# Seating the dilated heads in opposite halves of the partitions, and moving the rotation's angles to the first layer's down products

## The chip, the cores and the metric

One core of one Trainium2 chip. The metric is the device time of one execution in microseconds: the whole program, from the loading of the inputs to the writing of the output. Lower is better.

## The reference, cut to what matters

Two transformer blocks of two layers each, on 256 tokens of width 1024, in float32. The first block (called A in the kernel) has three kinds of attention and a gated feed-forward; the second (B) has pooling, a convolution, a dilated attention, a cross attention to a memory, and a feed-forward. What the change touches is the dilated attention of B and the rotation of its queries and keys:

```python
HEAD_DIM = 64
DIL_CONFIGS = ((128, 1), (512, 4), (2048, 16))
HEADS_PER_GROUP = 4
...
def rope_tables(positions):
    inv = ROPE_THETA_2 ** (-jnp.arange(0, ROT_DIM, 2, dtype=jnp.float32) / ROT_DIM)
    ang = positions.astype(jnp.float32)[..., None] * inv
    return jnp.cos(ang)[:, :, None, :], jnp.sin(ang)[:, :, None, :]
...
def dilated_attention(q, k, v):          # 12 heads: 3 groups of 4
    ...
    def block(bi):                       # 128 queries at a time
        for g, (window, dil) in enumerate(DIL_CONFIGS):
            ...                          # keys t, t - dil, ..., t - window; those before 0 masked out
            sc = jnp.einsum("bhqd,bhqkd->bhqk", qb[g], kk).astype(jnp.float32) * scale
            m = jnp.max(sc, axis=-1, keepdims=True)
            p = jnp.exp(sc - m)
            den = jnp.sum(p, axis=-1, keepdims=True)
            o = jnp.einsum("bhqk,bhqkd->bhqd", p, vv.astype(jnp.float32)) / den
            lses.append(m + jnp.log(den))
        wts = jax.nn.softmax(jnp.stack(lses, axis=0), axis=0)
        return jnp.sum(wts * jnp.stack(outs, axis=0), axis=0).astype(q.dtype)
```

Head h of the result mixes head h of each of the three groups, so the kernel takes those three together as one softmax over all their keys.

## The kernel before, in words

The activations lie with features on the partitions and tokens in the free dimension. Every weight is streamed once per layer through five raw buffers, in chunks of up to 128x1536 words, in an order fixed by hand. ScalarE copies a chunk to a rounded high part (`weights_hi`, `split_hi`, L641), VectorE subtracts that from the raw chunk to get the low part (`weights_lo`, `split_lo`, L652) and so frees the raw buffer for SP's next transfer. Four pairs of high and low parts are held. TensorE makes each product as three matmuls per 128x128 block of weights (L787, L789, L790: high by low, low by high, high by high), and frees a pair of parts when it leaves its chunk; ScalarE's split of the chunk four places later waits for that.

Each engine walks the same list of steps, `order_a` for the layers of block A and `order_b` for those of B, and issues its own share of each step. A step `("job", name)` is one product; on VectorE and ScalarE it begins with the splits up to two chunks beyond the job's last one. So what stands ahead of a job in the list stands ahead of its splits on VectorE.

In block A the attention runs as ten pairs of heads: `pair_in(i)` is the scores of pair i and, on TensorE, the turning of the probabilities of pair i - 1 (L1130, L1140), `pair_out(i)` the values of pair i - 2 (L1156). Behind pair_out 8, 9 and 10 stand the products `part0`, `part1`, `part2` (the output projection, as far as its inputs are there). Ahead of `part0` stands `("angles", 0)`: in layer 0, `vector_angles` (L2621 on) turns the positions to float and works out the angles of block B's rotation, reduced to -pi..pi, in a chain of instructions on 128x256 of which each waits for the one before. Their results lie in `ANG` and `TURNS` (named sin_dil and cos_dil in the trace) until ScalarE takes the sines at the end of block A. The last products of a layer are `down0` to `down3`, 44 blocks of weights each; behind each of them VectorE adds the product to x (L1714). The chunk borders of `down2` and `down3` run through without a cut, so `down2` is three full chunks and two thirds of a fourth.

In block B the queries and keys of the twelve dilated heads lie in `QKB` (qk_b): twelve tiles of 256 columns, six of queries and six of keys, and in each tile two heads, one in partitions 0 to 63 and one in 64 to 127. Head f (group g, head h: f = 4g + h) lies in tile f // 2, half f % 2. The sixteen score steps (eight per layer: head h, query block m) stand between the twelve `gate` products. A step makes three matmuls with a contraction of 64 (`tensor_dil_scores`, L1915), one for each group: 128 queries by the keys seen so far, 128 of them for m = 0 and 256 for m = 1. All three have f % 2 = h % 2. Groups 0 and 1 go to the first score bank and group 2 to the second. Then VectorE scales and masks them into `PB` (L1961), ScalarE takes the exponentials, VectorE divides, TensorE turns the result (L1927) and multiplies it with the values (L1943), each a step later:

```python
            for g in range(NG):
                f = g * DH + h
                r = slice((f % 2) * DHD, (f % 2 + 1) * DHD)
                ins = nc.tensor.matmul(dil_scores(h, m, g), QKB[r, f // 2, m * P:(m + 1) * P],
                                       QKB[r, 6 + f // 2, 0:dil_tiles(m) * P], start=True, stop=True)
```

`dil_columns` says which columns of w_in make up a tile of `QKB`: the sixteen turned elements of both heads stand together in the middle of the partitions. The weights are laid out so on the host.

Of the kernel before, what the change touches and what calls it, by code (L numbers as in the profile page):

```python
# [15 lines left out]
P = 128  # L16
DM = 1024
T = 256
QT = T // P
# [30 lines left out]
NG = len(DILS)  # L50
DH, DHD = 4, 64
# [23 lines left out]
def dil_columns(first, tile):  # L75

    turned = [(r + half * ROT // 2, 1) for r in range(ROT // 2) for half in range(2)]
    heads = [first + (2 * tile + half) * DHD for half in range(2)]
    return [(heads[0] + ROT, DHD - ROT)] + [(h + r, n) for h in heads for r, n in turned] + [(heads[1] + ROT, DHD - ROT)]


def constants():
# [45 lines left out]
    return at, np.ascontiguousarray(np.concatenate(list(cols.values()), 1))  # L128

# [272 lines left out]
def transformer(nc, known, stream_a, jobs_a, stream_b, jobs_b, const_at,  # L404
                x_in, mem_in, pos_in, w_a, w_b, gains_a, gains_b, consts, out):
    ctx = ExitStack()
    with ctx:
# [122 lines left out]
        QKB = b1.place("qk_b", (12, T))  # L530
# [7 lines left out]
        PB = b1.place("probs_b", (NG, QT, P))  # L538
# [42 lines left out]
        score_bank = [ctx.enter_context(nc.psum_tensor(f"scores{i}", [P, PAIR], F32)) for i in range(2)]  # L581
# [440 lines left out]
        n = KF // 2 - 1  # L1022
        order_a += [("ffn_hi", n - 1), ("ffn_in", n), ("ffn_lo", n - 1), ("ffn_out", n), ("ffn_hi", n), ("ahead", f"up{n}"), ("ffn_lo", n)]
        order_a += [("job", "down0"), ("root_table", "down")] + [("job", f"down{i}") for i in range(1, 4)]

# [623 lines left out]
        def vector_a(dve, l):  # L1649
# [4 lines left out]
            for kind, name in order_a:  # L1654
# [4 lines left out]
                if kind == "front":  # L1659
                    tag, i = name  # L1660
# [12 lines left out]
                elif kind == "angles":  # L1673
                    if l == 0:
                        vector_angles(dve)
# [29 lines left out]
                elif kind == "job":  # L1705
# [5 lines left out]
                    elif name[0] == "o" or name.startswith("down"):  # L1711
                        i = int(name[-1])
# [178 lines left out]
        def dil_tiles(m):  # L1891

            return m + 1

        def dil_scores(h, m, g):

            w = dil_tiles(m) * P
            return score_bank[g // 2][:, (g % 2) * w:(g % 2 + 1) * w]

# [4 lines left out]
        def tensor_dil_scores(pe, l, i):  # L1904
            s = B
            h, m = D_STEPS[i]
            if i == 0:
                pe.wait_ge(*s.at(l, "qk_rope", 2))
                pe.wait_ge(*s.at(l, "values", "v0"))
            else:  # L1910
                pe.wait_ge(*s.at(l, "dil_masked", i - 1))
            for g in range(NG):
                f = g * DH + h
                r = slice((f % 2) * DHD, (f % 2 + 1) * DHD)
                ins = nc.tensor.matmul(dil_scores(h, m, g), QKB[r, f // 2, m * P:(m + 1) * P],  # L1915
                                       QKB[r, 6 + f // 2, 0:dil_tiles(m) * P], start=True, stop=True)
            ins.then_inc(*s.mark("dil_scores", i))
# [30 lines left out]
        def vector_dil(dve, l, i):  # L1948
# [7 lines left out]
            mask = const_b("mask").rearrange("p (g k n) -> p g k n", g=NG, k=QT)  # L1956
            for g0, gn in ((0, 2), (2, 1)):
                src = score_bank[g0 // 2][:, 0:gn * kts * P].rearrange("p (g n) -> p g n", g=gn)
                dst = PB[:, g0:g0 + gn, 0:kts, :].rearrange("p g k n -> p g (k n)")
                mk = mask[:, g0:g0 + gn, QT - kts:QT, :].rearrange("p g k n -> p g (k n)")  # L1960
                ins = nc.vector.scalar_tensor_tensor(out=dst, in0=src, scalar=DHD ** -0.5, in1=mk, op0=ALU.mult, op1=ALU.add)  # L1961
# [658 lines left out]

        def vector_angles(dve):  # L2621

            dve.wait_ge(loaded["pos"], 16)
            nc.vector.tensor_copy(ANG[:, :], POS[:, :]).then_inc(*O.mark("angle", 0))
            dve.wait_ge(*O.at(0, "angle", 0))
            nc.vector.tensor_scalar(ANG[:, :], ANG[:, :], const("inv_freq"), None, ALU.mult).then_inc(*O.mark("angle", 1))
# [131 lines left out]
```

## Time and profile before

| | |
|---|---|
| median of 3 runs | 1678.62 us |
| lowest, highest | 1677.86, 1681.99 us |
| the profiled execution | 1683.09 us, its span 1681.3 |
| TensorE matmul busy | 1641.5 us (98%) |
| TensorE weight load busy | 1585.0 us (94%) |
| VectorE, ScalarE, GpSimd busy | 1202.8, 900.3, 113.7 us |
| HBM read | 271.13 MB, 162 GB/s over the span |
| granted TensorE clock, mean | 0.995 |

The profile is one execution of the program. An engine's busy time is the time in which it executes an instruction; TensorE's matmuls overlap, so the distance from the start of one to the start of the next says more than the duration of one. A row of a timeline gives the start, the time covered, the engine, the line, what it writes and reads, how many records were merged, and in brackets the idle time before it with what ended it. A float32 matmul leaves two records, one for each pass. The rows of fp32r products (L787, L789, L790) leave one.

### The profile page before, as it was taken

How to read it: one execution, taken by the hardware profiler on the slowest of the kernel's cores; microseconds unless marked ns; L12 is line 12 of the kernel's file. 1: busy time of each engine (PE TensorE's matmuls, PEld its weight loads, DVE VectorE, ACT ScalarE, POOL GpSimd, SP SyncE). 2: the span in 40 equal slices, each digit the busy share in tenths (PEclk: the TensorE clock that was granted, in tenths of full speed). 3: DMA queues.
4: the chain of work that ended last, by engine and by line, in shares of the span. 5: the costliest groups of instructions: out<-in, count | busy, mean ns of one | idle time of the engine just before them, and what ended most of it. 6: DMA issues, size and time to landing. Idle time of an engine off the chain costs nothing.

```text
span 1681.3 us, 31825 instructions
## 1 busy us (share of the span) xinstructions
PE 1641.5 (98%) x13566; PEld 1585.0 (94%) x13566; DVE 1202.8 (72%) x1765; ACT 900.3 (54%) x1378; POOL 113.7 (7%) x72
## 2 busy tenths in 40 slices
PE   9989999999999999999999999999999999999997
PEld 9978999999789999989999989999999999999997
DVE  5887777556977776477858768983677768679863
ACT  5585644454675444544545665544445446655542
POOL 2020000020110000210000110001200001110000
PEclk9999999999999999999999999999999999999999
DMA  8313555553225555555335435554454345345550
GB/s 294 109 59 114 196 197 189 173 194 126 95 86 183 202 201 182 211 203 189 114 134 189 136 125 195 198 193 165 165 197 162 132 155 184 120 151 207 197 184 34
DMA packets 53406, 275.03 MB, mean 164 GB/s; under 512 B 6288, under 2 KB 6928, under 8 KB 53136
## 3 DMA queue, kind: packets, MB, share of 16 engines
q1 hardware_dynamic: 52544, 271.15, 46.3%
q8 instruction: 107, 1.75, 0.4%
q10 hardware_dynamic: 720, 1.84, 0.3%
q14 instruction: 35, 0.29, 0.0%
HBM read 271.13 MB, written 1.05 MB: 162 GB/s over the span
## 4 chain that ended last, share of the span: by engine, by line
PE 75%; DVE 16%; ACT 5%; issue 2%; POOL 1%; DMA 0%; ACTq 0%; SPq 0%; DVEq 0%; POOLq 0%
PE bank L787 16%; PE bank L789 15%; PE bank L790 15%; DVE weights_lo L652 4%; PE scores L787 3%; PE scores L789 3%; PE scores L790 3%; PE heads L787 2%; PE heads L790 2%; PE heads L789 2%; ACT weights_hi L641 1%; DVE x_lo L934 1%; PE scores L1915 1%; ACT probs L1205 1%; PE heads L1943 1%
## 5 line engine op out<-in xcount | busy, mean ns | idle before, releaser
L652 DVE TENSOR_TENSOR weights_lo<-raw,weights_hi 128x1536 fp32r<-128x1536 f32 (+2 forms) x344 | 583.8, 1716 | 226.8 <-ACT weights_hi L641 226.4
L641 ACT ACTIVATE weights_hi<-raw 128x1536 fp32r<-128x1536 f32 (+4 forms) x352 | 499.9, 1440 | 179.5 <-PE bank L790 82.7
L787 PE MATMUL bank<-x_hi,weights_lo 128*128 128x256 f32 (+1 forms) x1588 | 443.7, 279 | 2.5 <-DVE weights_lo L652 2.1
L789 PE MATMUL bank<-x_lo,weights_hi 128*128 128x256 f32 (+1 forms) x1588 | 440.3, 277 | 0.0
L790 PE MATMUL bank<-x_hi,weights_hi 128*128 128x256 f32 (+1 forms) x1588 | 440.3, 277 | 0.0
L787 PEld LDWEIGHTS bank<-x_hi,weights_lo 128*128 128x128 f32 (+1 forms) x1588 | 297.4, 187 | 6.5 <-DVE weights_lo L652 2.8
L789 PEld LDWEIGHTS bank<-x_lo,weights_hi 128*128 128x128 f32 (+1 forms) x1588 | 296.9, 187 | 0.1
L790 PEld LDWEIGHTS bank<-x_hi,weights_hi 128*128 128x128 f32 (+1 forms) x1588 | 296.5, 187 | 0.0
L787 PE MATMUL bank<-hidden_hi,weights_lo 128*128 128x256 f32 x692 | 191.5, 277 | 0.4 <-DVE hidden_lo L2254 0.4
L789 PE MATMUL bank<-hidden_lo,weights_hi 128*128 128x256 f32 x692 | 191.1, 276 | 0.0
L790 PE MATMUL bank<-hidden_hi,weights_hi 128*128 128x256 f32 x692 | 191.1, 276 | 0.0
L787 PEld LDWEIGHTS bank<-hidden_hi,weights_lo 128*128 128x128 f32 x692 | 130.0, 188 | 0.7 <-DVE hidden_lo L2254 0.6
L789 PEld LDWEIGHTS bank<-hidden_lo,weights_hi 128*128 128x128 f32 x692 | 129.9, 188 | 0.0
L790 PEld LDWEIGHTS bank<-hidden_hi,weights_hi 128*128 128x128 f32 x692 | 129.9, 188 | 0.0
L787 PE MATMUL scores<-x_hi,weights_lo 128*128 128x256 f32 x416 | 115.5, 278 | 0.9 <-DVE weights_lo L652 0.9
L789 PE MATMUL scores<-x_lo,weights_hi 128*128 128x256 f32 x416 | 115.3, 277 | 0.0
L790 PE MATMUL scores<-x_hi,weights_hi 128*128 128x256 f32 x416 | 115.3, 277 | 0.0
L846 POOL TENSOR_TENSOR squares<-squares 128x512 f32<-128x512 f32 x28 | 51.7, 1846 | 821.5 <-ACT squares L2183 630.5
L787 PEld LDWEIGHTS scores<-x_hi,weights_lo 128*128 128x128 f32 x416 | 78.5, 189 | 1.2 <-issue 1.2
L789 PEld LDWEIGHTS scores<-x_lo,weights_hi 128*128 128x128 f32 x416 | 78.1, 188 | 0.0
L790 PEld LDWEIGHTS scores<-x_hi,weights_hi 128*128 128x128 f32 x416 | 78.1, 188 | 0.0
L787 PE MATMUL heads<-x_hi,weights_lo 128*128 128x256 f32 x256 | 71.4, 279 | 0.5 <-DVE weights_lo L652 0.5
(427 smaller groups left out, 3427.4 us busy)
## 6 DMA issues: line engine op xcount, KB each, us to landing
raw<-in_w_b SPq DMA_DIRECT2D x194, 768.0 KB, 4.2
raw<-in_w_a SPq DMA_DIRECT2D x120, 768.0 KB, 4.2
raw<-in_w_a SPq DMA_DIRECT2D x16, 512.0 KB, 3.4
raw<-in_w_b SPq DMA_DIRECT2D x10, 512.0 KB, 4.0
raw<-in_w_b SPq DMA_DIRECT2D x2, 752.0 KB, 4.5
raw<-in_w_a SPq DMA_DIRECT2D x2, 736.0 KB, 8.2
raw<-in_w_b SPq DMA_DIRECT2D x2, 720.0 KB, 5.0
raw<-in_w_a SPq DMA_DIRECT2D x2, 672.0 KB, 6.9
```

Source lines behind the costliest of these rows:

```text
L641: nc.scalar.activation(whi[c % SPLIT][:, 0:n], raw[c % RAW][:, 0:n], ACT.Copy).then_inc(*s.mark("weights_hi", c))
L652: nc.vector.tensor_tensor(wlo[c % SPLIT][:, 0:n], raw[c % RAW][:, 0:n], whi[c % SPLIT][:, 0:n].bitcast(F32), ALU.subtract).then_inc(*s.mar ...
L787: ins = nc.tensor.matmul(dst, wl, xh, start=start, stop=False, skip_group_check=skip)
L789: nc.tensor.matmul(dst, wh, xl, start=False, stop=False, skip_group_check=skip)
L790: ins = nc.tensor.matmul(dst, wh, xh, start=False, stop=stop, skip_group_check=skip)
L846: nc.gpsimd.tensor_tensor(sq[:, 0:2, :], sq[:, 0:2, :], sq[:, 2 * n:2 * n + 2, :], ALU.add).then_inc(*s.mark("sq_pairs", (tag, n)))
L934: nc.vector.scalar_tensor_tensor(out=XL[:, k, :], in0=X[:, k, :], scalar=gains(k), in1=XH[:, k, :].bitcast(F32), op0=ALU.mult, op1=ALU.sub ...
L1205: ins = nc.scalar.activation(PA[c][:, m, :], score_bank[c][:, m * T:(m + 1) * T], ACT.Exp, scale=f[:, m:m + 1], bias=ROW[:, r + m:r + m + ...
L1915: ins = nc.tensor.matmul(dil_scores(h, m, g), QKB[r, f // 2, m * P:(m + 1) * P], QKB[r, 6 + f // 2, 0:dil_tiles(m) * P], start=True, stop= ...
L1943: ins = nc.tensor.matmul(out_bank[rows, m * P:(m + 1) * P], VB[:, kt, f * DHD:(f + 1) * DHD], PTB[:, g * kts + kt, :], start=(n == 0), sto ...
```

## The change

The twelve heads get seats of their own, in a table: tiles 0 to 3 each hold one head of group 0 and one of group 1, with group 0 in the lower half for even h and in the upper for odd h; tiles 4 and 5 hold the heads of group 2 in order. So in each score step groups 0 and 2 stand in one half and group 1 in the other. Groups 0 and 2 go to the first score bank, group 1 to the second, and the mask instructions pair groups 0 and 2. The values keep their places. And the angles: the conversion of the positions stays behind pair_out 8, all the rest moves behind `down1` of layer 0.

```diff
@@ dil_columns
-    heads = [first + (2 * tile + half) * DHD for half in range(2)]
+    heads = [first + f * DHD for f in SEATS[tile]]
@@ new
+SEATS = [(h, DH + h) if h % 2 == 0 else (DH + h, h) for h in range(DH)] + [(2 * DH + h, 2 * DH + h + 1) for h in range(0, DH, 2)]
+
+def seat(f):
+
+    return next((t, heads.index(f)) for t, heads in enumerate(SEATS) if f in heads)
@@ order_a
-        order_a += [("job", "down0"), ("root_table", "down")] + [("job", f"down{i}") for i in range(1, 4)]
+        order_a += [("job", "down0"), ("root_table", "down"), ("job", "down1"), ("angles", 1), ("job", "down2"), ("job", "down3")]
@@ vector_a
                 elif kind == "angles":
-                    if l == 0:
+                    if l == 0 and name == 0:
+                        vector_positions(dve)
+                    elif l == 0:
                         vector_angles(dve)
@@ dil_scores
-            return score_bank[g // 2][:, (g % 2) * w:(g % 2 + 1) * w]
+            return score_bank[g % 2][:, (g // 2) * w:(g // 2 + 1) * w]
@@ tensor_dil_scores
-                f = g * DH + h
-                r = slice((f % 2) * DHD, (f % 2 + 1) * DHD)
-                ins = nc.tensor.matmul(dil_scores(h, m, g), QKB[r, f // 2, m * P:(m + 1) * P],
-                                       QKB[r, 6 + f // 2, 0:dil_tiles(m) * P], start=True, stop=True)
+                tile, half = seat(g * DH + h)
+                r = slice(half * DHD, (half + 1) * DHD)
+                ins = nc.tensor.matmul(dil_scores(h, m, g), QKB[r, tile, m * P:(m + 1) * P],
+                                       QKB[r, 6 + tile, 0:dil_tiles(m) * P], start=True, stop=True)
@@ vector_dil
-            for g0, gn in ((0, 2), (2, 1)):
-                src = score_bank[g0 // 2][:, 0:gn * kts * P].rearrange("p (g n) -> p g n", g=gn)
-                dst = PB[:, g0:g0 + gn, 0:kts, :].rearrange("p g k n -> p g (k n)")
-                mk = mask[:, g0:g0 + gn, QT - kts:QT, :].rearrange("p g k n -> p g (k n)")
+            for g0, gn in ((0, 2), (1, 1)):
+                src = score_bank[g0][:, 0:gn * kts * P].rearrange("p (g n) -> p g n", g=gn)
+                dst = PB[:, g0:NG:2, 0:kts, :].rearrange("p g k n -> p g (k n)")
+                mk = mask[:, g0:NG:2, QT - kts:QT, :].rearrange("p g k n -> p g (k n)")
@@ vector_angles, split in two
-        def vector_angles(dve):
+        def vector_positions(dve):
             dve.wait_ge(loaded["pos"], 16)
             nc.vector.tensor_copy(ANG[:, :], POS[:, :]).then_inc(*O.mark("angle", 0))
+
+        def vector_angles(dve):
+
             dve.wait_ge(*O.at(0, "angle", 0))
```

VectorE in the attention of layer 0, behind pair_out 8 (the two splits are those that `part1` needs), before:

```order
L1194 TENSOR_TENSOR mix_lo<-heads,mix_hi 128x256 [waits mix_hi]
L2624 CAST sin_dil<-positions 128x256 [waits loaded_pos]
L2626 TENSOR_SCALAR sin_dil<-sin_dil,const 128x256 [waits angle]
L2629 TENSOR_SCALAR cos_dil<-sin_dil 128x256 [waits angle]
L2631 TENSOR_SCALAR cos_dil<-cos_dil 128x256 [waits turns]
L2633 TENSOR_SCALAR cos_dil<-cos_dil 128x256 [waits turns]
L2641 SCALAR_TENSOR_TENSOR sin_dil<-cos_dil,sin_dil 128x256 [waits turns]
L2641 SCALAR_TENSOR_TENSOR sin_dil<-cos_dil,sin_dil 128x256 [waits angle] x3
L2645 TENSOR_SCALAR sin_dil<-sin_dil 128x256 [waits angle]
L2648 TENSOR_SCALAR cos_dil<-sin_dil 128x256 [waits reduced]
L2650 TENSOR_TENSOR cos_dil<-cos_dil,sin_dil 128x256 [waits abs]
L2652 TENSOR_SCALAR cos_dil<-cos_dil 128x256 [waits abs]
```

and now:

```order
L1202 TENSOR_TENSOR mix_lo<-heads,mix_hi 128x256 [waits mix_hi]
L2634 CAST sin_dil<-positions 128x256 [waits loaded_pos]
L660 TENSOR_TENSOR weights_lo_58<-raw_49,weights_hi_54 128x1536 [waits weights_hi]
L660 TENSOR_TENSOR weights_lo_59<-raw_50,weights_hi_55 128x1536 [waits weights_hi]
L1177 TENSOR_REDUCE row<-scores 128x2 [waits map_scores,map_exp]
```

Before, the same two splits (at L652) followed behind the last of the twelve; now they follow on the conversion.

VectorE in layer 0 behind the addition of `down1`, now (four splits follow the block, of the third and fourth chunk of `down2` and the next two; the first of them is shown):

```order
L1724 TENSOR_TENSOR x<-x,bank 128x512 [waits filled]
L2639 TENSOR_SCALAR sin_dil<-sin_dil,const 128x256 [waits angle]
L2642 TENSOR_SCALAR cos_dil<-sin_dil 128x256 [waits angle]
L2644 TENSOR_SCALAR cos_dil<-cos_dil 128x256 [waits turns]
L2646 TENSOR_SCALAR cos_dil<-cos_dil 128x256 [waits turns]
L2654 SCALAR_TENSOR_TENSOR sin_dil<-cos_dil,sin_dil 128x256 [waits turns]
L2654 SCALAR_TENSOR_TENSOR sin_dil<-cos_dil,sin_dil 128x256 [waits angle] x3
L2658 TENSOR_SCALAR sin_dil<-sin_dil 128x256 [waits angle]
L2661 TENSOR_SCALAR cos_dil<-sin_dil 128x256 [waits reduced]
L2663 TENSOR_TENSOR cos_dil<-cos_dil,sin_dil 128x256 [waits abs]
L2665 TENSOR_SCALAR cos_dil<-cos_dil 128x256 [waits abs]
L660 TENSOR_TENSOR weights_lo_60<-raw_50,weights_hi_56 128x1536 [waits weights_hi]
```

Before, the four splits followed straight on the addition; now all twelve moved instructions stand between.

TensorE at the second score step of layer 0 of block B (m = 1), before:

```order
L790 MATMUL bank0<-x_hi_67,weights_hi3_57 128x256
L1915 MATMUL scores0<-qk_b_110 128x256 [waits dil_masked]
L1915 MATMUL scores0<-qk_b_110 128x256
L1915 MATMUL scores1<-qk_b_110 128x256
L1927 MATMUL turned0<-const_84,probs_b_118 128x128 [waits dil_weights]
```

and now:

```order
L798 MATMUL bank0<-x_hi_67,weights_hi3_57 128x256
L1925 MATMUL scores0<-qk_b_110 128x256 [waits dil_masked]
L1925 MATMUL scores1<-qk_b_110 128x256
L1925 MATMUL scores0<-qk_b_110 128x256
L1937 MATMUL turned0<-const_84,probs_b_118 128x128 [waits dil_weights]
```

The order of the groups is the same; the banks and the halves of the rows now go first, second, first. Nothing else moves on any engine.

## Rows read from the trace of the kernel before

**Rows 1.** The page: busy time of TensorE, and the chain that ended last.
```profile
PE 1641.5 (98%) x13566; PEld 1585.0 (94%) x13566; DVE 1202.8 (72%) x1765; ACT 900.3 (54%) x1378; POOL 113.7 (7%) x72
...
PE 75%; DVE 16%; ACT 5%; issue 2%; POOL 1%; DMA 0%; ACTq 0%; SPq 0%; DVEq 0%; POOLq 0%
```

**Rows 2.** Timeline of TensorE, 141 to 152 us (layer 0, block A).
```profile
141.80 0.38 PE L1156 MATMUL heads<-merge_part,mla_v 128*64 128x256 f32 x1
145.00 0.36 PE L787 MATMUL bank<-mix_hi,weights_lo 128*128 128x256 f32 x1 [2.82 <-DVE weights_lo L652]
...
151.49 0.71 PE L1140 MATMUL turned<-const,probs 128*128 128x128 f32 x5
```

**Rows 3.** Timeline of VectorE, 138 to 150.5 us.
```profile
138.25 0.28 DVE L2624 CAST sin_dil<-positions 128x256 f32<-128x256 int32 x1
138.57 0.35 DVE L2626 TENSOR_SCALAR sin_dil<-sin_dil,const 128x256 f32<-128x256 f32 x1
...
143.11 3.42 DVE L652 TENSOR_TENSOR weights_lo<-raw,weights_hi 128x1536 fp32r<-128x1536 f32 x2
...
149.95 0.62 DVE L1182 TENSOR_SCALAR probs<-probs,row 128x256 f32<-128x256 f32 x2
```

**Rows 4.** Windows: length, busy TensorE, weight load, VectorE, ScalarE, GpSimd; clock; DMA, GB/s.
```profile
142.00:145.90 3.90, 1.08 (x9) 0.93 (x8) 3.80 (x6) 0.00 (x0) 0.00 (x0) 1.00 0.04 8
145.90:149.30 3.40, 3.40 (x19) 3.40 (x18) 2.76 (x8) 1.88 (x7) 0.00 (x0) 0.50 0.78 234
384.80:391.70 6.90, 6.90 (x34) 6.90 (x34) 3.75 (x8) 1.58 (x2) 0.00 (x0) 0.51 0.28 103
32.00:45.00 13.00, 13.00 (x116) 13.00 (x115) 6.45 (x8) 4.71 (x19) 0.00 (x0) 1.00 0.55 188
```

**Rows 5.** Timeline of TensorE, first two score steps of block B.
```profile
795.12 0.93 PE L1915 MATMUL scores<-qk_b 64*128 64x128 f32 x6
795.98 0.38 PE L787 MATMUL bank<-x_hi,weights_lo 128*128 128x256 f32 x1
...
801.63 1.56 PE L1915 MATMUL scores<-qk_b 64*128 64x256 f32 x6
803.12 0.33 PE L1927 MATMUL turned<-const,probs_b 128*128 128x128 f32 x1
```

**Rows 6.** Timeline of TensorE, score matmuls of block A: halves alternating, then 96 rows.
```profile
79.54 1.14 PE L1130 MATMUL scores<-qk 64*128 64x256 f32 x8
80.61 0.39 PE L796 MATMUL bank<-weights_hi,x_lo 128*128 128x256 f32 x1
...
122.66 1.89 PE L1130 MATMUL scores<-qk 96*128 96x256 f32 x8
124.39 0.27 PE L1140 MATMUL turned<-const,probs 128*128 128x128 f32 x1
```

**Rows 7.** Windows over the score steps of both layers of block B.
```profile
790.00:880.00 90.00, 90.00 (x724) 84.05 (x723) 62.34 (x88) 45.76 (x66) 0.00 (x0) 1.00 0.40 139
1280.00:1370.00 90.00, 90.00 (x724) 84.04 (x723) 60.79 (x87) 44.09 (x66) 0.00 (x0) 1.00 0.38 135
```

**Rows 8.** Timeline of VectorE behind `down1` of layer 0, block A.
```profile
326.63 0.69 DVE L1714 TENSOR_TENSOR x<-x,bank 128x512 f32<-128x512 f32 x1 [3.46 <-PE bank L790]
327.24 3.42 DVE L652 TENSOR_TENSOR weights_lo<-raw,weights_hi 128x1536 fp32r<-128x1536 f32 x2
```

**Rows 9.** Timeline of ScalarE, 329 to 348 us.
```profile
330.77 1.49 ACT L641 ACTIVATE weights_hi<-raw 128x1536 fp32r<-128x1536 f32 x1 [2.47 <-PE bank L790]
334.85 1.49 ACT L641 ACTIVATE weights_hi<-raw 128x1536 fp32r<-128x1536 f32 x1 [2.59 <-PE bank L790]
...
343.01 0.63 ACT L641 ACTIVATE weights_hi<-raw 128x512 fp32r<-128x512 f32 x1 [2.59 <-PE bank L790]
347.50 1.06 ACT L641 ACTIVATE weights_hi<-raw 128x1024 fp32r<-128x1024 f32 x1 [3.86 <-DMA raw<-in_w_a]
```

**Rows 10.** The page: transfers of block A's weights, KB each, us from issue to landing.
```profile
raw<-in_w_a SPq DMA_DIRECT2D x120, 768.0 KB, 4.2
```

## The prediction

> **What bounds the kernel now.** I read the page first: TensorE shows 98% busy, and three quarters of the chain that ended last are its own matmuls [rows 1]. So an edit counts for what it takes off TensorE's queue, or out of one of its few waits. The waits of TensorE came next, then the timelines around them. One wait is in the middle of the block that this change moves: at 141.80 us the last value products of pair 7 start, and the next instruction, the first product of `part1`, starts only at 145.00, with 2.82 us of idle time that ended when VectorE delivered `weights_lo` [rows 2]. VectorE's own timeline shows why that split was late: `CAST`, then twelve small instructions on 128x256, each waiting for the one before, from 138.57 to 143.11, and only then the two splits [rows 3]. The granted clock tells the rest: full in 142.0 to 145.9, where TensorE was busy for 1.08 of 3.9 us, and 0.50 (its level of 1.2 GHz instead of 2.4) in 145.9 to 149.3 [rows 4]. The second place is TensorE's own time: in the sixteen steps of the dilated attention the three score matmuls stand in the same half of the rows and run one after another [rows 5].
>
> **The angles leave the attention.** `CAST` stays (0.3 us). The twelve others leave; by start times they hold VectorE for 143.11 - 138.57 = 4.54 us [rows 3]. The first split then starts at 138.57 and ends 3.42 / 2 = 1.71 us later, at 140.3, before TensorE is through with the value products at about 142.2. Hence the idle 2.82 us go whole. With TensorE fed, nothing is left of what preceded the fall of the clock, and 3.4 us at 0.50 would have taken 1.7 at full clock: 2.8 + 1.7 = 4.5 us. Behind it VectorE, whose softmax of pair 9 ended at 149.95 + 0.62 [rows 3], is earlier by 4.54 too, and TensorE, which took those probabilities at 151.49 [rows 2], by 4.5: the next meeting keeps its slack of 0.9 us, and ScalarE's splits between them start earlier with it. So I take the gain whole: **-4.5 us**. Bounds: 2.8 if the clock would have stayed up in the run that is timed, or falls all the same; 4.54 is all that VectorE can give. SP's queue waits for buffers that VectorE frees, so the transfers move with it.
>
> **The angles enter the down products.** In layer 0 they now stand behind the addition of `down1`, ahead of four splits of `down2`. The addition ends at 327.3 and the splits follow from 327.24 on [rows 8]. With 4.54 us put in, they start at 331.8, and the first ends at 333.5. When does TensorE want it? ScalarE's split at 334.85 waited for TensorE to leave the chunk four places earlier [rows 9]; that is the second chunk of `down2`, so TensorE steps onto the third, the one that is late, at that moment. Slack: 334.85 - 333.5 = 1.3 us. The next split ends at 335.2, and a chunk lasts 4.1 us (334.85 - 330.77 in the same rows), so it is wanted at 338.9; the two after it have more. What is queued behind the block is only these splits. They free the raw buffers 4.5 us later, so SP issues the transfer that reuses the first of them at 333.5 instead of 329.0; a full chunk lands in 4.2 us [rows 10], 337.7, and ScalarE splits that one, the last of `down3`, only at 343.01 [rows 9]. The next layer's first chunk, for which ScalarE waited on a DMA until 347.50 [rows 9], reuses a buffer that is freed behind the addition of `down2`, a whole product later, when VectorE is long level again. **0 us**; with the cover gone it would be the excess over 1.3 us.
>
> **The heads' seats.** A score matmul is two passes in the trace, so a step has six. A step with one key tile takes 795.98 - 795.12 = 0.86 us from its first pass to the next instruction, one with two takes 803.12 - 801.63 = 1.49 [rows 5]; there are eight of each, 18.8 us. The first block has both ways of doing it on record: eight passes of 256 columns on 96 rows, one after another, take 124.39 - 122.66 = 1.73 us, 0.216 each; eight passes on 64 rows in alternating halves take 80.61 - 79.54 = 1.07, four times 0.216 and 0.2 for changing form at both ends [rows 6]. The old step fits: 6 x 0.216 + 0.2 = 1.50. After the change groups 0 and 2 share one half and group 1 has the other, so the fuller half has four passes: 4 x 0.216 + 0.2 = 1.06, 0.43 less. With one key tile a pass is (0.86 - 0.2) / 6 = 0.11, so 0.64, 0.22 less. 8 x 0.43 + 8 x 0.22 = **-5.2 us**. TensorE has no idle time in either stage: 90.00 us busy of 90, at full clock, with VectorE busy 62 us and DMA at 40% [rows 7], so what it saves nobody takes back. Bounds: no row shows alternating halves with 128 columns, where each pass needs a weight load twice as often; nothing there would leave 3.4. Nothing at all is the lower end. I take the full 5.2, since the nearest row is the same form with the same two banks. VectorE's mask instructions only pair groups 0 and 2 instead of 0 and 1, with the same elements: 0, and VectorE's idle third covers what it could be. The permuted weight columns are packed on the host, and the transfers keep their size: 0.
>
> A rule is to be weighed here. The trace's own pair of forms, 1.73 against 1.07 us [rows 6], gives a factor of 1.6 with the changes of form in it. The Trainium skill (TensorEngine Tiling (Array Packing), section Overview) promises up to 2x for a contraction of 64 or less; by it the step would lose three of its six passes, 7.8 us in all instead of 5.2, and the sum would be -12.3 (its price is worked out under the rivals). This case's rows speak for less, since two of the three heads stay in one half.
>
> **Sum.** -4.5 + 0 - 5.2 = -9.7 us. The profiled execution took 1683.1 us (span 1681.3), so it would take 1673.4. The median of the three timed runs is 1678.6, 4.5 lower. The profiled one lost 1.7 us to the clock at 145.9 and 3.4 at 384.8 (6.9 us at 0.51), while the same work in layer 0 (32 to 45 us) had full clock [rows 4]; so such falls are not fixed by the program, and the gap may be just that. Taken off the median: 1668.9, rounded to 1669; if the median run had no fall at 145.9, 1670.6. The Trainium skill (TensorE: Matmul & The Clock Gate, Part 1) says that the number of slow matmuls of one kernel varies from run to run; the two rows just named agree.
>
> **Rivals.** A measurement tells this kernel from no change at about 0.3%, 5.0 us, so the border is 1673.6.
> - *Both parts work* (as above): 1669, from 1665.5 (a fall of 3.4 us also gone) to 1671. Chance 0.76.
> - *No overlap of the halves*, because the third matmul or the order of the passes keeps the array from taking the second half early: only the angles count, 1678.6 - 4.5 = 1674.1. Against: the 1.07 us of rows 6. For: there two full pairs alternate, here there are three matmuls. 0.08. The other way in which the change doesn't do what it says, overlap with 256 columns but not with 128: 1670.7, 0.05.
> - *A full halving*: a step has three slots instead of six passes, so 3 x 0.216 = 0.65 us less with two key tiles and 3 x 0.11 = 0.33 with one, 8 x 0.65 + 8 x 0.33 = 7.8: 1678.6 - 4.5 - 7.8 = 1666.3. Against: groups 0 and 2 use the same rows and the same bank, so each step keeps four passes in one half. 0.03. (The rule of the Trainium skill's page TensorEngine Tiling (Array Packing), Overview, is this case.)
> - *The angles' new place costs*: the third chunk of `down2` comes later than 334.85 because the block runs slower than 4.54 us there; up to 2 us of idle time, 1671 to 1672, 0.05.
> - *Slower than before: the clock falls in the score steps.* Place: the sixteen score steps, in the two stretches of rows 7. Work in two halves at once counts, to whatever grants the clock, as less work, and after some of the steps it falls to the lower level. Price: 1.7 us a fall, as at 145.9, so from six falls on (10.2 us) the gain is gone; at all sixteen 1678.6 - 9.7 + 27 = 1696. For it: the clock did fall after a thin stretch [rows 4]. Against: that stretch had 2.8 us of idle time, and here TensorE stays full; the paired halves of rows 6 stand in a stretch of full clock. 0.03.
>
> **Numbers.** Likeliest 1669. Low end 1665 (both parts and 3.4 us of clock, or the full halving), high end 1674.5 (the angles alone). Below 1673.6 lie 0.76 + 0.05 + 0.03 + most of 0.05: faster 0.88. The angles alone give "within 0.3%": 0.09. Slower: 0.03.
>
> **What the changed profile would show.** Right: no idle time before the products of `part1`, clock 1.00 there, splits from 138.6 on; in the down products the block of twelve behind `down1`, four splits right behind it, and TensorE without a gap near 330 (old 334.85); score steps of 0.64 and 1.06 us with the passes starting in pairs; TensorE's busy time about 7 us less. Wrong: steps still at 0.86 and 1.49; a wait of TensorE for `weights_lo` in `down2`; a clock row of 0.50 near 790 to 870. The sum would also be wrong if the time drops by 4.5 in the first layer and the second layer's start gives it back in a wait for DMA.

## The result and the profile after

The changed kernel takes 1669.93 us (median of 4 runs, 1669.03 to 1672.83) against 1678.86 for the kernel before (4 runs in the same comparison): 8.9 us less, a ratio of 0.9949 with a 95% interval of 0.9937 to 0.9961, that is 6.5 to 10.6 us. The forecast was 1669.0 in a range of 1665.0 to 1674.5. The profiled execution of the changed kernel took 1672.8 us (span 1671.0), 10.3 less than the profiled one of before.

The page, busy time and chain, to be read beside [rows 1]:

```profile
PE 1633.4 (98%) x13566; PEld 1577.4 (94%) x13566; DVE 1202.3 (72%) x1765; ACT 900.0 (54%) x1378; POOL 114.1 (7%) x72
...
PE 76%; DVE 15%; ACT 4%; issue 2%; POOL 1%; DMA 0%; ACTq 0%; SPq 0%; DVEq 0%; POOLq 0%
```

TensorE is busy 8.1 us less with the same 13566 matmuls; the other engines do what they did.

**The attention of layer 0.** TensorE and VectorE (timelines, the places of [rows 2] and [rows 3]):

```profile
143.31 0.38 PE L1164 MATMUL heads<-merge_part,mla_v 128*64 128x256 f32 x1
143.61 0.38 PE L795 MATMUL bank<-mix_hi,weights_lo 128*128 128x256 f32 x1
...
148.52 1.06 PE L1148 MATMUL turned<-const,probs 128*128 128x128 f32 x8
```

```profile
139.75 0.28 DVE L2634 CAST sin_dil<-positions 128x256 f32<-128x256 int32 x1
140.79 3.42 DVE L660 TENSOR_TENSOR weights_lo<-raw,weights_hi 128x1536 fp32r<-128x1536 f32 x2 [0.75 <-ACT weights_hi L649]
...
147.64 0.62 DVE L1190 TENSOR_SCALAR probs<-probs,row 128x256 f32<-128x256 f32 x2
```

The 2.82 us in brackets of [rows 2] are gone: the first product of `part1` starts 0.3 us behind the last value products. The first split now waits 0.75 us for ScalarE's high part; before, the angles covered that. From the last value products to the turning of pair 9 it takes 148.52 - 143.31 = 5.21 us, where the kernel before took 151.49 - 141.80 = 9.69: 4.5 us less. Windows over the same place, and over the stretches of [rows 4]:

```profile
141.40:144.80 3.40, 3.40 (x28) 2.61 (x27) 3.40 (x3) 0.72 (x1) 0.00 (x0) 1.00 0.34 110
381.90:388.70 6.80, 6.80 (x46) 6.80 (x46) 4.31 (x9) 1.58 (x2) 0.00 (x0) 0.75 0.34 117
32.00:45.00 13.00, 13.00 (x105) 13.00 (x104) 6.45 (x8) 4.71 (x19) 0.00 (x0) 0.89 0.53 190
```

No fall of the clock behind `part1`. But this execution had one in 32 to 45 us, where the one of before had none, and half as long a one at 384.

**The down products of layer 0**, VectorE and then ScalarE, beside [rows 8] and [rows 9]:

```profile
323.82 0.69 DVE L1724 TENSOR_TENSOR x<-x,bank 128x512 f32<-128x512 f32 x1 [3.46 <-PE bank L798]
324.43 0.35 DVE L2639 TENSOR_SCALAR sin_dil<-sin_dil,const 128x256 f32<-128x256 f32 x1
...
328.75 0.29 DVE L2665 TENSOR_SCALAR cos_dil<-cos_dil 128x256 f32<-128x256 f32 x1
328.96 6.76 DVE L660 TENSOR_TENSOR weights_lo<-raw,weights_hi 128x1536 fp32r<-128x1536 f32 x4
```

```profile
332.04 1.49 ACT L649 ACTIVATE weights_hi<-raw 128x1536 fp32r<-128x1536 f32 x1 [2.58 <-PE bank L798]
```

The chain takes 328.96 - 324.43 = 4.53 us, the first split ends at 328.96 + 6.76 / 4 = 330.65, and TensorE steps onto that chunk at 332.04: 1.4 us to spare. The waits of TensorE from 300 to 360 us have one entry, the 0.8 us at the next layer's start.

**The score steps**, TensorE's timeline, beside [rows 5]:

```profile
790.17 0.71 PE L1925 MATMUL scores<-qk_b 64*128 64x128 f32 x6
790.81 0.38 PE L795 MATMUL bank<-x_hi,weights_lo 128*128 128x256 f32 x1
...
796.47 1.13 PE L1925 MATMUL scores<-qk_b 64*128 64x256 f32 x6
797.52 0.44 PE L1937 MATMUL turned<-const,probs_b 128*128 128x128 f32 x2
...
862.24 1.52 PE L1953 MATMUL heads<-probs_tb,v_b 128*64 128x128 f32 x12
```

A step takes 790.81 - 790.17 = 0.64 us with one key tile and 797.52 - 796.47 = 1.05 with two (0.86 and 1.49 before; the single records give 1.06). The starts of the single records show two passes at a time for the first two slots, 0.007 us apart, and the last two passes alone.

**A ledger of the two profiled executions**, from the starts of the same instructions. The changed one is 1.5 us late when the attention's value products end (143.31 against 141.80), which is its clock fall near 42 us. At the addition of `down1` it is 2.8 us early (323.82 against 326.63): 4.3 of the angles' 4.5 are left. At the first score step it is 4.95 early (790.17 against 795.12): 1.7 of the 2.1 between are the shorter fall at 384. At the layer's last value products, which in the kernel before started at 869.58, it is 7.3 early: 2.4 from one layer's eight steps. The second layer brings 2.4 again, 0.5 came between the two stages from products that no edit touched, and the end is 10.3 early. The change itself accounts for 4.3 + 4.8 = 9.1 of it.

### The profile page after: what moved, and what is told of

Its sections match the earlier page's. It is cut to its first block, busy times and chain, and to the rows that moved or that the text cites. A ratio compares the mean times of both kernels' runs of the same rounds, so it can differ in the third digit from the quotient of the medians.

```text
span 1671.0 us, 31825 instructions
## 1 busy us (share of the span) xinstructions
PE 1633.4 (98%) x13566; PEld 1577.4 (94%) x13566; DVE 1202.3 (72%) x1765; ACT 900.0 (54%) x1378; POOL 114.1 (7%) x72
## 3 DMA queue, kind: packets, MB, share of 16 engines
HBM read 271.13 MB, written 1.05 MB: 163 GB/s over the span
## 4 chain that ended last, share of the span: by engine, by line
PE 76%; DVE 15%; ACT 4%; issue 2%; POOL 1%; DMA 0%; ACTq 0%; SPq 0%; DVEq 0%; POOLq 0%
PE bank L795 16%; PE bank L797 16%; PE bank L798 16%; DVE weights_lo L660 4%; PE scores L795 3%; PE scores L797 3%; PE scores L798 3%; PE heads L795 2%; PE heads L798 2%; PE heads L797 2%; ACT weights_hi L649 1%; DVE x_lo L942 1%; PE heads L1953 1%; DVE x L2414 1%; ACT probs L1213 1%
```

## The experiments

The times of the experiments are medians beside the kernel before on the same chip (1679.8 us in the session of e1 to e4, 1682.2 in that of e5 to e8). The ratios are what compares.

### e1: the angles alone

The kernel before with this part of the diff:

```diff
-        order_a += [("job", "down0"), ("root_table", "down")] + [("job", f"down{i}") for i in range(1, 4)]
+        order_a += [("job", "down0"), ("root_table", "down"), ("job", "down1"), ("angles", 1), ("job", "down2"), ("job", "down3")]
...
-                    if l == 0:
+                    if l == 0 and name == 0:
+                        vector_positions(dve)
+                    elif l == 0:
                         vector_angles(dve)
```

> The kernel before with the twelve angle instructions moved behind down1 of layer 0, the seats left alone. Theory (the angles held up the split that part1 waits for, and the idle time pulled the clock down): 4.3 to 4.6 us faster than before, 2.8 of it the idle time before part1 and 1.7 the clock; TensorE's row before part1 shows no idle time, score steps stay at 0.86 and 1.49 us. Rival (VectorE's lead is given back at the next wait or at the DMA wait of the second layer's start): 0 to 2 us faster. Rival (the clock falls elsewhere instead): 2.6 to 3.0 us faster.

Measured: ratio 0.9971, interval 0.9961 to 0.9981, 3.2 to 6.5 us faster with 4.9 in the middle. The waits of TensorE from 130 to 180 us no longer have `part1`'s (us in total, times, longest):

```profile
PE scores L1130 <- ACT probs L1205: 0.9, 1, 0.9
PE scores L737 <- ACT x_hi L902: 0.5, 1, 0.5
PE heads L787 <- DVE weights_lo L652: 0.2, 1, 0.2
```

The score steps stayed at 0.86 and 1.49. The gain is not given back at the next layer's start: by the starts of the same instructions e1 is 4.1 us early at 200 us and at 356 us. Both rivals, up to 3.0 us, lie outside the interval. The third line is new against before: 0.2 us of the gain return as a wait further on.

### e2: the seats alone

The changed kernel with the chain of angles put back:

```diff
-                 8: [("angles", 0), ("job", "part0")], 9: [("job", "part1")], 10: [("job", "part2")]}
+                 8: [("angles", 0), ("angles", 1), ("job", "part0")], 9: [("job", "part1")], 10: [("job", "part2")]}
...
-        order_a += [("job", "down0"), ("root_table", "down"), ("job", "down1"), ("angles", 1), ("job", "down2"), ("job", "down3")]
+        order_a += [("job", "down0"), ("root_table", "down")] + [("job", f"down{i}") for i in range(1, 4)]
```

> The changed kernel with all the angle instructions back behind pair_out 8, so that only the seats and banks differ from before. Theory (two of three score matmuls overlap, TensorE is the bound in both stages): 4.6 to 5.2 us faster than before, steps of 0.64 and 1.06 us; the two parts add up to what both did together (8.9 us). Rival (part of the gain is lost to other engines inside the stage): under 4 us although the steps are as short. The idle 2.8 us before part1 are back.

Measured: ratio 0.9970, interval 0.9959 to 0.9980, 5.0 us faster; steps of 0.64 and 1.06. The product of the ratios of e1 and e2 is 0.9941, that of the whole change 0.9949: the parts add up within their intervals. The rival of under 4 us is not excluded by the median, whose interval is 3.4 to 6.9 us. It is excluded by the starts: in e2 the seats bring 2.41 us in each layer, as in all the other executions that have them.

This execution also shows something that e1 can't: the stall without the fall of the clock. Its timeline of TensorE and its windows, then its waits from 130 to 180 us:

```profile
145.30 0.38 PE L1164 MATMUL heads<-merge_part,mla_v 128*64 128x256 f32 x1
148.47 0.36 PE L795 MATMUL bank<-mix_hi,weights_lo 128*128 128x256 f32 x1 [2.79 <-DVE weights_lo L660]
...
154.29 1.06 PE L1148 MATMUL turned<-const,probs 128*128 128x128 f32 x8 [0.81 <-ACT merge_part L1222]
```

```profile
145.50:149.40 3.90, 1.11 (x10) 0.96 (x9) 3.80 (x6) 0.00 (x0) 0.00 (x0) 1.00 0.03 8
149.40:152.80 3.40, 3.40 (x33) 3.40 (x32) 2.76 (x8) 1.92 (x7) 0.00 (x0) 1.00 0.74 230
```

```profile
PE bank L795 <- DVE weights_lo L660: 2.8, 1, 2.8
...
PE turned L1148 <- ACT merge_part L1222: 0.8, 1, 0.8
```

The same idle time as in [rows 2], the same thin window as in [rows 4], and full clock behind it. And yet TensorE doesn't keep the 1.7 us: it comes to the turning of pair 9 early and waits there 0.8 us for ScalarE's copies, a wait that the kernel before did not have, since at half clock TensorE arrived late enough. From the last value products to that turning e2 takes 154.29 - 145.30 = 8.99 us, against 9.69 before. So with the clock up the chain of VectorE and ScalarE sets the pace behind the stall, and between these two executions the fall costs 0.7 us, not 1.7.

### e3: the banks alone

The kernel of e1 with the banks and the mask of the change, heads in their old halves:

```diff
-            return score_bank[g // 2][:, (g % 2) * w:(g % 2 + 1) * w]
+            return score_bank[g % 2][:, (g // 2) * w:(g // 2 + 1) * w]
...
-            for g0, gn in ((0, 2), (2, 1)):
+            for g0, gn in ((0, 2), (1, 1)):
```

> The kernel of e1 with the banks of the three groups as in the change (first, second, first) and the mask instructions pairing groups 0 and 2, but all three heads still in the same half of the rows. Theory (the halves do it, the bank only has to be another one): steps stay at 0.86 and 1.49 us and the time is that of e1 within 0.5 us. Rival (the alternation of the banks itself brings the overlap): steps of 0.64 and 1.06 us, 5 us faster than e1. Rival (VectorE's mask instructions with the strided groups cost something): slower than e1 by the difference in the rows of the mask line times its count, at most 1 us.

Measured: ratio 0.9977 (0.9964 to 0.9990), that of e1 within the intervals. TensorE's timeline:

```profile
796.74 1.56 PE L1917 MATMUL scores<-qk_b 64*128 64x256 f32 x6
798.23 0.44 PE L1929 MATMUL turned<-const,probs_b 128*128 128x128 f32 x2
```

1.49 us, six passes one after another: the banks alone do nothing, the halves do it. (Whether the halves overlap when they share one bank, no run tries.) VectorE's mask in the four steps of one layer with two key tiles, grouped by form (the old pairing took 686 ns by the same view of before):

```profile
L1963 DVE SCALAR_TENSOR_TENSOR probs_b<-scores,const_b 128x512 f32<-128x512 f32 x4 | 2.7, 685 | 2.2 <-PE turned L1929 2.2
```

The pairing of groups 0 and 2 costs nothing here. By the starts e3 neither gains nor loses against the kernel before in either layer's score steps.

### e4: the order of the groups

```diff
-            for g in range(NG):
+            for g in (0, 2, 1):
                 tile, half = seat(g * DH + h)
```

> The changed kernel with the score matmuls of a step issued in the order group 0, group 2, group 1: the two heads of one half first, then the one of the other half. Theory A (each half works through its own passes, whichever comes first in the program): steps of 0.64 and 1.06 us as in the change, same time. Theory B (passes start in program order, so the second half can only start when the last matmul of the first half has started): five slots instead of four, 0.75 and 1.28 us, 2.6 us slower than the change. Theory C (only neighbours pair up, and passes of the pair alternate): 0.64 and 1.06 again, but with the pair at the end of the step, the single passes first.

Measured: ratio 0.9945 (0.9931 to 0.9959), as the change. The step has the same length although two matmuls of one half are now issued first:

```profile
796.65 1.13 PE L1925 MATMUL scores<-qk_b 64*128 64x256 f32 x6
797.71 0.44 PE L1937 MATMUL turned<-const,probs_b 128*128 128x128 f32 x2
```

The single records tell A from C. The pair stands at the start of the step, as in the change (starts at 796.652 and 796.666, then 796.972 and 796.986, then 797.188 and 797.404), and the record with the increment of `dil_scores`, which belongs to the last matmul of the program, is the one that starts at 796.986, ahead of two others. So each half works through its own matmuls, and the last one issued overtook the second. That is theory A; B and C fall.

One would then fear that the semaphore comes before the scores of group 2 are there. VectorE's timeline in the first step of e4, and the same of the changed kernel:

```profile
790.47 0.69 DVE L2487 TENSOR_TENSOR gates<-bank,y 128x512 f32<-128x512 f32 x1 [1.08 <-PE bank L798]
791.12 0.62 DVE L1971 SCALAR_TENSOR_TENSOR probs_b<-scores,const_b 128x256 f32<-128x256 f32 x2
```

```profile
790.28 0.69 DVE L2487 TENSOR_TENSOR gates<-bank,y 128x512 f32<-128x512 f32 x1 [1.08 <-PE bank L798]
790.92 0.62 DVE L1971 SCALAR_TENSOR_TENSOR probs_b<-scores,const_b 128x256 f32<-128x256 f32 x2
```

In e4 the record with the increment ends at 790.86 and the last record of the step at 791.07; the mask starts at 791.12. In the change both are one record, ending at 790.88, and the mask starts at 790.92. So the mask starts 0.04 to 0.05 us after the last record, whichever carries the increment, and the second layer's first step does the same. VectorE itself only just gets there in time: where nothing holds it up, a mask starts 0.60 us behind the start of `gates`; here it is 0.64 in the change and 0.65 in e4, so each waited some 0.04 to 0.05 us. Had e4's increment come with its own record, 0.2 us earlier, there would have been nothing to wait for. That fits an increment that waits for all that was issued before. But the evidence is two steps and 0.05 us, with modelled ends of the matmuls; in the others VectorE comes later anyway.

### e5 to e7: how much the down products hide

> The changed kernel once more, to have it beside the next three on the same chip: 8 to 10 us faster than before.

Measured: ratio 0.9942 (0.9928 to 0.9957).

e6 and e7 put n = 3 and n = 14 more instructions ahead of the chain:

```diff
         def vector_angles(dve):
 
+            for n in range(3):
+                nc.vector.tensor_scalar(TURNS[:, :], ANG[:, :], 1.0, None, ALU.mult).then_inc(*O.mark("turns", ("pad", n)))
+                dve.wait_ge(*O.at(0, "turns", ("pad", n)))
```

> The changed kernel with three more instructions of the same kind (128x256, each waiting for the one before) at the head of the angle chain behind down1, so 1.0 us more on VectorE there. In the changed kernel's profile the first split behind the chain ends at 330.65 and TensorE steps onto its chunk at 332.04, 1.4 us later. Theory (the down products hide the chain, with that much to spare): no idle time of TensorE in down2, time as the change within 0.5 us. Rival (the spare time is less than it looks, because the split has to be there before the matmul that needs it by more than the rows show): some tenths of idle time at the third chunk of down2.

Measured: ratio 0.9947 (0.9931 to 0.9963). VectorE's and ScalarE's timelines:

```profile
329.63 6.76 DVE L660 TENSOR_TENSOR weights_lo<-raw,weights_hi 128x1536 fp32r<-128x1536 f32 x4
```

```profile
331.73 1.49 ACT L649 ACTIVATE weights_hi<-raw 128x1536 fp32r<-128x1536 f32 x1 [2.58 <-PE bank L798]
```

The first split ends at 331.32, 0.4 us before TensorE wants it, and TensorE's waits have no entry in `down2`. The slack is what the rows say.

> The same with fourteen more, about 4.6 us. Theory: TensorE waits 4.6 - 1.4 = 3.2 us for the split of the third chunk of down2, and nothing of it is won back before the end of the layer, since TensorE is the bound there: 3.2 us slower than the change, up to 4.9 if the clock falls after the wait. Rival (the next layer's start waits for a DMA anyway and swallows it): under 1 us slower. This is also what the change would have cost if its chain were twice as long.

Measured in place, TensorE's timeline and the windows:

```profile
334.12 0.39 PE L795 MATMUL bank<-hidden_hi,weights_lo 128*128 128x256 f32 x1 [3.42 <-DVE weights_lo L660]
```

```profile
330.70:334.50 3.80, 0.38 (x3) 0.39 (x4) 3.66 (x7) 1.48 (x1) 0.00 (x0) 1.00 0.00 0
334.50:337.90 3.40, 3.40 (x19) 3.40 (x18) 3.40 (x3) 0.00 (x0) 0.00 (x0) 0.50 0.26 77
32.00:45.00 13.00, 13.00 (x116) 13.00 (x115) 6.45 (x8) 4.70 (x19) 0.00 (x0) 1.00 0.53 190
```

A wait of 3.42 us where 3.2 was expected, and the clock falls behind it for 3.4 us, 1.7 lost. By the starts of the same instructions e7 is 1.2 us ahead of the changed kernel before the wait and 4.8 behind it at 358 us, so 6.05 in place: 5.3 for the wait and the fall, and 0.75 from products behind them that ran at the longer of two intervals (last section). The median hides it: ratio 0.9950 (0.9931 to 0.9968), only 1.3 us above e5 and within the intervals of one another. The expectation of "3.2 to 4.9 slower" failed as a statement on the median, and the profiled span, 1673.9 against 1671.7 for e5, is 2.2 above. The starts say where the rest went. e7 is 5.1 us behind e5 at 358 us and 5.0 at 1500 us, so the next layer's start swallows nothing; then it gets 2.8 back in the last feed-forward stage, which it ran at the shorter interval. It was also 1.0 ahead from the beginning, with full clock at 32 to 45 us (0.90 in e5). With four and six runs that scatter by 3 and 6 us, the medians cannot settle 3 us.

### e8: an attempt to beat both

In the changed kernel TensorE waits in the first layer of block B:

```profile
728.16 0.39 PE L795 MATMUL bank<-x_hi,weights_lo 128*128 128x256 f32 x1 [1.67 <-DVE weights_lo L660]
```

```diff
-                    ("mem_squares", 0), ("job", "q2"), ("job", "k2"), ("turn", 1), ("mem_mean", 0), ("job", "v0"), ("swap", 2), ("mem_factor", 0), ("job", "v1"), ("turn", 2),
-                    ("job", "a0"), ("job", "a1"), ("pool", 0), ("job", "bx01"), ("pool", 1), ("job", "bxb2"), ("pool", 2),
+                    ("job", "q2"), ("job", "k2"), ("turn", 1), ("mem_squares", 0), ("job", "v0"), ("swap", 2), ("job", "v1"), ("turn", 2), ("mem_mean", 0),
+                    ("job", "a0"), ("mem_factor", 0), ("job", "a1"), ("pool", 0), ("job", "bx01"), ("pool", 1), ("job", "bxb2"), ("pool", 2),
```

> An attempt to be faster than both. In block B's first layer TensorE waits 1.67 us for a low part at 726.5 (profile of the change), because ScalarE squares the memory (2.2 us) before it splits the next chunk, and 0.36 us for GpSimd's sums of those squares. Here the squares stand behind the product k2 and TensorE's two short steps on them behind v1 and a0. Theory (ScalarE's order makes both waits): both go, 2.0 us faster than the change. Rival (the wait is made by VectorE's turn and ScalarE's swap DMAs that stand ahead as well): 0 to 0.7 us. Rival (the squares now hold up the split for v1 or a0 and the wait only moves): no change, with a new wait of 1 to 2 us near 735 to 750.

Measured: ratio 0.9933 (0.9919 to 0.9947), the lowest of all, 1671.2 us against 1673.3 for e5 in the same session. The intervals of the two overlap. In place it is plain. From the first product of block B to the first score step it takes, in e8 and then in the change:

```profile
695.31 0.36 PE L745 MATMUL bank<-x_hi,weights_lo 128*128 128x256 f32 x1 [0.83 <-DVE x L1724]
...
787.42 0.71 PE L1925 MATMUL scores<-qk_b 64*128 64x128 f32 x6
```

```profile
695.20 0.36 PE L745 MATMUL bank<-x_hi,weights_lo 128*128 128x256 f32 x1 [0.82 <-DVE x L1724]
```

787.42 - 695.31 = 92.11 us against 790.17 - 695.20 = 94.97: 2.9 us less, of which the two waits are 2.0; where the other 0.9 came from was not traced. No new wait came. So the squares on ScalarE made the first wait. The second, 0.36 us for GpSimd's sums of the squares, went too, but TensorE's own steps on them also moved later, so this run doesn't say which move removed it.

## Why the prediction was right, and where its terms were off

**The bound.** Right: TensorE's own time and its waits were what counted. 4.8 us came off its score steps and 2.8 off its waits, and of this the other engines took back one wait of 0.2. Its busy time fell by 8.1 us where about 7 was forecast.

**The angles leave (forecast 4.5).** Right in place and mechanism: the split waited for the chain, the idle time went whole, and at the turning of pair 9 TensorE is 9.69 - 5.21 = 4.5 us earlier, 2.9 of it from before the first product and 1.6 from products at full clock. Then 0.2 go back in a wait, so 4.3 are left; e1 gives 4.9 with an interval that holds both. The lower bound of 2.8, for a run without the fall, was too low: e2 is such a run, and against it the change takes 8.99 - 5.21 = 3.8 us less, the idle time and the later wait of 0.8.

**"The next meeting keeps its slack of 0.9".** Wrong: none is left, without harm. ScalarE's timeline, the last copies of what TensorE had turned before, in the change and then in e2:

```profile
147.77 0.61 ACT L1222 ACTIVATE merge_part<-turned 128x512 f32<-128x512 f32 x1
```

```profile
153.53 0.61 ACT L1222 ACTIVATE merge_part<-turned 128x512 f32<-128x512 f32 x1
```

In e2 the turning of pair 9 waits for these copies and starts 154.29 - 154.14 = 0.15 us behind their end. In the change it starts 148.52 - 148.38 = 0.14 behind it, so the two engines arrive together; in the kernel before it was 0.8. What the step missed is the split: it now waits 0.75 us for ScalarE's high part, so VectorE's softmax of pair 9, counted from the last value products, is only (149.95 - 141.80) - (147.64 - 143.31) = 3.8 us earlier, not 4.54, and ScalarE's copies with it. Any more and the gain would have shrunk; that it stayed whole is luck.

**The angles enter (forecast 0, slack 1.3).** Right: slack 1.4, no wait; e6 used up 1.0 of it without effect, e7 went over it and paid the excess and a fall of the clock.

**The seats (forecast 5.2).** Right in the steps: 0.64 and 1.05, from 0.86 and 1.49. Off by 0.2 us a layer in the stage: 2.4 instead of 2.6, because the product between the sixth and the seventh step ran with a longer interval from matmul to matmul (0.118 us instead of 0.113) than before. It isn't chance: all seven executions with the seats gain 2.41 us in each layer. Why the product runs slower is open. The rule of the Trainium skill (TensorEngine Tiling (Array Packing), Overview), up to 2x, did not apply in full: four slots for six passes, as the rows of the first block had said.

**The rivals.** "No overlap" and "not with 128 columns" are excluded by the steps; so is the full halving. The clock did not fall in any score step (1.00 in both stages), which takes away the one way to a slower kernel. That the angles' new place costs is excluded by TensorE's waits.

**Against the median.** The forecast took 9.7 off 1678.6 and came to 1669; measured were 8.9 and 1669.9. The terms in place give 9.1. That the median agrees as closely is in part luck, since its interval runs from 6.5 to 10.6 us; the terms are borne out by the starts, not by the median. Nor is it the clock that makes the profiled pair differ by 10.3: the change's fall near 42 us and its shorter fall at 384 are 1.7 us each and cancel. The remark that the gap between profiled and timed runs may be just the clock's was too narrow: five executions of e5 with the same mean clock, 0.997, lie between 1670.5 and 1676.6 us. The last section names a second source of the same size.

## What to carry to other kernels

Where three matmuls with a contraction of 64 stand side by side, seat their operands so that the fuller half has as few as can be, and count the passes of the fuller half: that number, times the interval, plus 0.2 us for the change of form, was the step to within 0.01 us. Here each half had a bank of its own; whether it needs one was not tried. Work that nobody waits for soon belongs where its engine idles; to find the room, take the moment at which the consumer frees the buffer that the late part's successor needs, and subtract. And before you add the clock to a stall's idle time, look for the next meeting with another engine. This stall of 2.8 us was worth 4.5 where the clock fell behind it and 3.8 where it didn't.

## What the runs showed of the hardware that was not expected

**Two speeds at full clock.** In long runs of products, TensorE goes from one matmul to the next in 0.113 us or in 0.118, both at a granted clock of 1.00, and can keep to one for a hundred microseconds. The last feed-forward stage, windows of the changed kernel and then of e4, which differ there in no instruction:

```profile
1505.00:1605.00 100.00, 100.00 (x850) 100.00 (x851) 90.30 (x128) 53.54 (x63) 0.00 (x0) 1.00 0.56 196
```

```profile
1505.00:1600.00 95.00, 95.00 (x838) 95.00 (x839) 88.93 (x126) 52.68 (x61) 0.00 (x0) 1.00 0.60 201
```

100 / 850 = 0.118 and 95 / 838 = 0.113. In e3 and e4 the whole stage is 3.2 us shorter for it by the starts of the same instructions, in e7 2.8. The executions of before, of the change, e1, e2, e5, e6 and e8 had the slow form there, e3, e4 and e7 the fast one, and e8 had it in the other layer as well. That is as much as e8's edit and over half of either part of this change, and may be part of why runs of the same kernel scatter by 3 to 10 us; what chooses the form was not found out.

**The program alone does not fix where the clock falls.** After nearly the same thin stretch of 3.9 us (TensorE busy 1.08 and 1.11 us), the clock fell to its lower level in the kernel before and stayed up in e2. In 32 to 45 us, before anything differs, it was 1.00 in the kernel before and in e7, 0.89 in the change and 0.90 in e5. The Trainium skill (TensorE: Matmul & The Clock Gate, Part 1) says that the count of slow matmuls of one kernel varies from run to run; these pairs agree. (The two rows that the prediction named beside it stand in one execution, so they could not show it.) What makes the difference is open.

**Halves overtake one another.** In e4 a matmul issued last started its passes before one issued ahead of it in the other half. The same page of the Trainium skill (Part 3: Packing small matmuls — row/col tiling) has matmuls strictly in program order in start and end; for two-pass float32 matmuls in opposite halves the starts differ from that here, and so do the modelled ends (790.86 for the last one issued, 791.07 for the one before it). The page's conclusion, that one increment on the last matmul is sound, fits the two steps of e4 that bear on it.
